# Attention: VectorE copies the second group's turned blocks of the second head

## The reference, cut to what matters

```
logits = q @ k.T * 64**-0.5 + bias        # masked to the chosen keys
p      = softmax(logits, axis=-1)
out    = (p @ v) * silu(gate)
```

## Time and profile before

| what | us |
|---|---|
| median of 3 runs | 965.35 (964.88 to 966.65) |
| the profiled execution's own time | 965.28 |
| its span, first to last instruction | 963.4 |
| TensorE busy in the span | 940.8 (98%) |
| VectorE busy | 645.3 (67%) |
| ScalarE busy | 529.8 (55%) |
| GpSimd busy | 342.2 (36%) |

### The profile page before, as it was taken

The page is one execution under the profiler, slowest core; times in us unless marked ns, Lnnn a source line. Parts: engine busy times, 40 slices in busy tenths (PEclk is TensorE's granted clock), DMA queues, the critical chain, the costliest instruction groups (busy, mean ns, idle before and its releaser), DMA issues.

```text
span 963.4 us, 15067 instructions
## 1 busy us (share of the span) xinstructions
PE 940.8 (98%) x5642; PEld 777.2 (81%) x5642; DVE 645.3 (67%) x1104; ACT 529.8 (55%) x912; POOL 342.2 (36%) x437
## 2 busy tenths in 40 slices
PE   7999999999999999999999899999999999999997
PEld 5888899988787877777776688888888888888886
DVE  5348899699799865455565836664487593989152
ACT  6647788868665445555565743333373543684211
POOL 0022265467777535243323651103231222226100
PEclk9999999999999999999999999999999999999999
DMA  9515222011332332123124342212212111113062
GB/s 346 181 45 77 50 57 59 3 44 33 97 79 88 113 119 89 44 81 108 55 100 157 117 154 102 92 68 87 66 44 65 45 44 44 44 45 132 1 218 87
DMA packets 70302, 83.88 MB, mean 87 GB/s; under 512 B 3480, under 2 KB 52696, under 8 KB 70232
## 3 DMA queue, kind: packets, MB, share of 16 engines
q1 hardware_dynamic: 68816, 81.33, 26.1%
q10 hardware_dynamic: 1416, 1.63, 1.5%
HBM read 64.07 MB, written 18.35 MB: 86 GB/s over the span
## 4 chain that ended last, share of the span: by engine, by line
PE 88%; DVE 4%; ACT 3%; issue 2%; POOL 1%; DMA 0%; DVEq 0%; POOLq 0%; ACTq 0%
PE ps L1841 24%; PE ps L1843 23%; PE ps L1842 23%; PE ps L1908 3%; PE ps L2101 3%; PE ps L1956 2%; PE ps L2117 2%; DVE prob L1584 1%; PE ps L1958 1%; PE ps L1957 1%; PE ps L2053 1%; POOL wL L719 1%; PE ps L2185 1%; PE ps L2028 0%; ACT pT L1167 0%
## 5 line engine op out<-in xcount | busy, mean ns | idle before, releaser
L1841 PE MATMUL ps<-hH,wH 128*128 128x512 f32 (+1 forms) x356 | 138.8, 390 | 0.2 <-POOL wL L719 0.2
L1843 PE MATMUL ps<-hH,wL 128*128 128x512 f32 (+1 forms) x356 | 135.6, 381 | 0.0
L1842 PE MATMUL ps<-hL,wH 128*128 128x512 f32 (+1 forms) x356 | 135.3, 380 | 0.0
L1841 PE MATMUL ps<-h1H,w_slot_H 128*128 128x512 f32 x256 | 99.8, 390 | 0.0
L1843 PE MATMUL ps<-h1H,w_slot_L 128*128 128x512 f32 x256 | 99.6, 389 | 0.0
L1842 PE MATMUL ps<-h1L,w_slot_H 128*128 128x512 f32 x256 | 99.6, 389 | 0.0
L1429 DVE TENSOR_SCALAR_CACHE_REDUCE junk<-score,cand 128x768 bf16<-128x768 f32 (+3 forms) x128 | 96.7, 809 | 1.1
L719 POOL TENSOR_TENSOR wL<-raw,wH 128x1024 fp32r<-128x1024 f32 x28 | 70.4, 2519 | 59.9 <-ACT wH L912 59.7
L716 POOL TENSOR_TENSOR w_slot_L<-raw,w_slot_H 128x1024 fp32r<-128x1024 f32 x16 | 41.3, 2587 | 125.1 <-ACT w_slot_H L908 125.1
L1841 PEld LDWEIGHTS ps<-hH,wH 128*128 128x128 f32 x356 | 67.0, 188 | 13.3 <-issue 0.7
L1843 PEld LDWEIGHTS ps<-hH,wL 128*128 128x128 f32 x356 | 66.9, 188 | 13.1
(11 more groups left out here) (302 smaller groups left out, 2345.3 us busy)
## 6 DMA issues: line engine op xcount, KB each, us to landing
raw<-in_even_w_in SPq DMA_DIRECT2D x28, 512.0 KB, 4.0
raw<-in_odd_w_in SPq DMA_DIRECT2D x16, 512.0 KB, 4.0
xn<-in_x SPq DMA_DIRECT2D x8, 512.0 KB, 10.7
gate_d<-gst SPq DMA_DIRECT2D x16, 256.0 KB, 2.2
xt<-in_x SPq DMA_DIRECT2D x8, 512.0 KB, 3.5
x_d<-xt SPq DMA_DIRECT2D x8, 512.0 KB, 2.6
raw_row<-in_odd_w_out SPq DMA_DIRECT2D x8, 512.0 KB, 3.2
xt<-x_d SPq DMA_DIRECT2D x8, 512.0 KB, 4.3
```

Of the source, the lines that this page charges most:

```text
L1841: pe.matmul(dst, lH, rH, start=k == 0, stop=False)
L1842: pe.matmul(dst, lH, rL, start=False, stop=False)
L1843: return pe.matmul(dst, lL, rH, start=False, stop=k == nk - 1)
```

## The change

The copy of the second group's blocks for head e = 1 goes from ScalarE to VectorE (`copied_by_dve`). There are 16 of them, in the steps named above, with 1 to 4 blocks of 128 columns. It has a semaphore of its own, `turn_out_dve`, and `turned_out(g, e)` tells TensorE which of the two to wait for and how high. On VectorE the copy stands between `masked(a, 0)` and `masked(a, 1)` in steps without filling (in steps 29 to 31 it stands ahead of the `gate_b` there), and behind `masked(a, 1)` in steps with filling. In step 32, which has no filling and no `masked`, it stands behind `inverses(31)` and ahead of `split_first_mix`. TensorE's order is unchanged.

```diff
+    def copied_by_dve(g, e):
+        return e == 1 and group_in_step(g) == 1
+
+    def turned_out(g, e):
+        mine = copied_by_dve(g, e)
+        order = [(i, k) for i in range(g + 1) for k in range(2) if (i, k) <= (g, e)]
+        return turn_out_dve if mine else turn_out, sum(copied_by_dve(*key) == mine for key in order)
...
             for g in groups:
                 for e in range(2):
-                    copy_turned(g, e)
+                    if not copied_by_dve(g, e):
+                        copy_turned(g, e)
...
+        def copy_turned_last(g):
+            m = BLOCKS[g][2]
+            dve.wait_ge(turn_full, 2 * g + 2)
+            if same_buffer_last(g) >= 0:
+                dve.wait_ge(pv_done, 2 * (same_buffer_last(g) + 1))
+            else:
+                for t in range(2):
+                    dve.wait_ge(gla_out[t], 8 * NT)
+                dve.wait_ge(bias_out, 16)
+            dve.tensor_copy(pT[1][:, 1, 0:m * P], ps[:, TURN_BANK[1], 0:m * P]).then_inc(turn_out_dve, 1)
...
+            second = blocks_of[a - 1][1:] if 1 <= a <= NW else []
             if a < NW:
                 masked(a, 0)
+            if not filler(a):
+                for g in second:
+                    copy_turned_last(g)
+            if a < NW:
                 if pieces_at(a)[0] is not None:
                     gate_b(pieces_at(a)[0])
                 masked(a, 1)
+            if filler(a):
+                for g in second:
+                    copy_turned_last(g)
...
                 if g:
-                    pe.wait_ge(turn_out, 2 * (g - 1) + e + 1)
+                    pe.wait_ge(*turned_out(g - 1, e))
...
-            pe.wait_ge(turn_out, 2 * g + 2)
+            for e in range(2):
+                pe.wait_ge(*turned_out(g, e))
```

More of the change, by code:

```diff
@@ L379, in build @@
     s_full, s_masked, max_ready, exp_done = ([sem(f"{n}{e}") for e in range(2)] for n in ("s_full", "s_masked", "max_ready", "exp_done"))
-    turn_full, turn_out, pv_done, out_done = sem("turn_full"), sem("turn_out"), sem("pv_done"), sem("out_done")
+    turn_full, turn_out, turn_out_dve = sem("turn_full"), sem("turn_out"), sem("turn_out_dve")
+    pv_done, out_done = sem("pv_done"), sem("out_done")
     rl_ready, rl_full = sem("rl_ready"), sem("rl_full")
```

## The result

The changed kernel takes 969.89 us (969.53 to 970.22, 4 runs) against 965.99 for the one before: ratio 1.005, 95% interval 1.0038 to 1.0062, so 3.7 to 6.0 us slower. The ratio is an estimate over single executions and not the quotient of the medians, which alone are 3.9 us apart. The forecast was 5.3 us slower, 970.6 us. Ratios here are taken over fast runs; two executions of the kernel before, at 1873.08 and 1043.85 us, are left out of them.

The account below looks back on a forecast made before the run. TensorE, busy 940.8 of 963.4 us, was taken to bound the kernel. Steps 5, 13, 21 (-0.5), steps 7, 15, 23 (+1.5), step 32 (+2.8) and clock (+1.5) gave +5.3 on 965.28: 970.6 us, range 966.5 to 973.3.

Parts of the forecast that it names:

- the 7.6 us: TensorE's wait at the turning for the first group's copies, which stay on ScalarE; claimed unchanged.
- Price of the copy: Time of a moved copy on VectorE: 0.29, 0.42, 0.55 and 0.69 us for 1 to 4 blocks.
- Steps 5, 13, 21: Attention steps with filling, 1 block: ScalarE loses a copy, next unit's logits come 0.17 us earlier each, -0.5 us.
- Steps 7, 15, 23: Steps without filling, 3 blocks: the copy delays masked(a, 1) and head 1's exponential, 0.5 us each, +1.5 us.
- Steps 8, 16, 24 and 29 to 31: Steps with 4-block copies and filling, and the late attention steps; claimed zero cost.
- Step 32: End of attention: copy first puts VectorE's low part behind GpSimd's last piece, output projection starts late, +2.8 us.
- The rule of the Trainium skill: Exclusive SBUF lock between VectorE and GpSimd; holding GpSimd for the high part too would add 0.3 us in step 32.
- The clock: Behind step 32's pause of 2.7 us TensorE runs 3 us at half speed, +1.5 us, ends 0 and 3.
- Sum: All terms together, passing through to the end of the kernel: +5.3 us, 970.6 us.

Follow-up runs that it names:

- kept: Changed kernel with the copies of steps 7, 15, 23 and 32 back on ScalarE; 965.19 us, ratio 1.0001 to the kernel before.
- last_act: Changed kernel with the copy of step 32 alone back on ScalarE; 966.04 us, ratio 1.0013 to the kernel before.
- busy: Changed kernel with 20 needless TensorE transposes between the last weighing and the output projection; 969.0 us, ratio 1.0047 to the kernel before.
- split_first: Changed kernel with step 32's copy behind VectorE's split of the first tile; 967.34 us, ratio 1.0023 to the kernel before.
- swap: Changed kernel with ScalarE making the second tile's high part before its last weight piece; 966.71 us, ratio 1.0012 to the kernel before.

## Why the prediction held

- *TensorE decides, and the 7.6 us are not for sale.* Right: the wait for ScalarE's copies at the turning is 7.6 us in 19 places after as before.
- *Price of the copy.* 0.29, 0.42, 0.56 and 0.69 us for 1 to 4 blocks, against 0.29, 0.42, 0.55 and 0.69 reckoned from two other instructions.
- *Steps 5, 13, 21: -0.17 each.* Right: TensorE's wait for the logits of unit 7 fell by 0.17 us, and by stretch A 0.14 a pair is left of it.
- *Steps 7, 15, 23: +0.5 each.* Right in place, a little high: 0.38, and TensorE's wait is 0.41 us, not 0.6. The copy starts 0.04 us behind the turning, not 0.10, and masked(7, 1) starts 0.47 us behind the copy's start, ahead of its recorded end. I had reckoned with the full duration.
- *Steps 8, 16, 24 and 29 to 31: nothing.* Right: B, which holds steps 29 to 31, is 41.66 where no fall came, against 41.64 before, and kept keeps the gain in A with the copies of steps 8, 16 and 24 on VectorE.
- *Step 32: +2.8.* Right: 2.75, by the mechanism named. It is shown from three sides: by taking the copy back (0), by letting VectorE's low part start ahead of GpSimd's piece (0.71), and by putting the copy behind the split (1.70).
- *The rule of the Trainium skill* ("SBUF — State Buffer", section "SBUF: two separate sides") that who starts first keeps the shared pair of ports for the whole instruction: the trace agrees for the low part, in both directions (3.27 us for the low part behind GpSimd, 2.73 for L721 behind the low part). Its consequence for the high part, GpSimd held until its end, is not seen: L721 began 0.16 us ahead of the high part's end and took 2.38 us, where the piece before it, with no instruction of VectorE beside it, took 2.36. The overlap is short, so this is a weak test. The prediction compared with a piece of 2.49 us as one with nothing beside it; the end of the low part lay beside that one, for 0.22 us.
- *The clock: +1.5.* Right in size where it comes (401.87 - 400.37), and it came in three profiles of four. The sum counted it as certain, and that was too strong: of two profiles of the same changed kernel one has it and the other not. That the execution compared here has it is in part luck. And the fall in step 27 of the profile before, my evidence that a pause brings one, cost that execution nothing: B is 41.64 with it and 41.65 without (last_act), because a wait of TensorE for VectorE behind it took up the loss (rows in the last section).
- *Sum +5.3.* The profiled execution shows +4.5. The difference is 0.35 us in steps 7, 15 and 23, less 0.1 in steps 5, 13 and 21, and 0.4 ahead of the attention, where nothing was changed and the twelve profiles spread over 2.7 us. The ratio leaves +3.7 to +6.0.

## What to carry to other kernels

An instruction that is moved to an idle engine is paid where it stands in that engine's line: between the two masked sums it cost 0.4 us because of what was queued behind it, and one of sixteen cost 2.75 us because it pushed an unrelated instruction behind a GpSimd instruction. Look first at the place where the engine's next result is awaited without slack, and there at what GpSimd runs beside a VectorE instruction with two inputs in SBUF. When an effect is below what medians can tell, cut the profiles at the same marks of the bounding engine: two stretches repeated to 0.1 us where whole runs of one kernel scattered by 1 to 4.

## What the runs showed of the hardware that I had not expected

The clock's falls move from one execution of a kernel to another. In steps 26 to 28 TensorE pauses three times for 0.8 to 1.2 us, and of the twelve profiles six have no fall there and six have 3.4, 6.8 or 10.2 us at half clock. What a fall cost depended on where it came. In the profile before it ran from 522.9 to 526.1, ahead of the last of the three pauses, and cost nothing: the logits of step 28, which wait 1.17 us for VectorE in last_act without a fall, started without a wait. First the profile before, then last_act, which is 0.84 us later from the start of B on:

```profile
527.73 0.41 PE L1956 MATMUL ps<-qkH 64*128 64x320 f32 x2
```

```profile
528.60 0.41 PE L1987 MATMUL ps<-qkH 64*128 64x320 f32 x2 [1.17 <-DVE small L1596]
```

In busy and split_first the fall of 3.4 us began behind the last pause and cost 1.3 us.

GpSimd and a VectorE instruction with two inputs in SBUF hold each other up. In the changed kernel GpSimd's L880 took 3.35 us with the low part of VectorE ahead of it; in swap and split_first it took 2.38 and 2.41 with none.
